# Low weight halves on GpSimd, four past-row pairs a block, rows out earlier and the compressed past kept on chip, in a hybrid conv and sparse-attention decoder step

## The reference, cut to what matters

```python
def even_project(x, w_in):                       # 1024 -> 3352 columns
    h = jnp.einsum('btd,de->bte', x, w_in)
    a_val, a_glu, a_gate, q, kv_c, kv_s, kv_w, g, b_gate = jnp.split(h, offsets, axis=-1)
    u = a_val * jax.nn.sigmoid(a_glu)
    ...
def conv_branch(u_ext, a_gate, conv_w, conv_b, ln_g, ln_b):     # 512 channels, width 31, causal
    y = lax.conv_general_dilated(u_ext, conv_w[:, None, :], (1,), 'VALID', ...) + conv_b
    return jax.nn.silu(layer_norm(y, ln_g, ln_b)) * jax.nn.silu(a_gate)

def compress_kv(kv, w_cmp):                      # 32 rows -> 1, stride 16
    ch = kv[:, :n_ch * CMP_STRIDE].reshape(B, n_ch, CMP_STRIDE, 2, KV_HEADS, HEAD_DIM)
    kc = (jnp.einsum('bnjchd,jchd->bnchd', ch[:, :-1], w_cmp[:CMP_STRIDE])
          + jnp.einsum('bnjchd,jchd->bnchd', ch[:, 1:], w_cmp[CMP_STRIDE:]))
    ...
def nsa_block(q, g, q_pos, kc, vc, kc_end, ks, vs, kw, vw, kw_pos):
    # three branches: compressed blocks, the 16 best blocks of 64 rows, the last 512 rows;
    # o = sigmoid(g)[0] * o_c + sigmoid(g)[1] * o_s + sigmoid(g)[2] * o_w
    ...
def mixer_out(a_out, b_out, b_gate, w_out):
    h = jnp.concatenate([a_out, b_out * jax.nn.silu(b_gate)], axis=-1)
    return jnp.einsum('bte,ed->btd', h, w_out)
```

## Time and profile before

| | us |
|---|---|
| runs | 1334.31, 1334.58, 1342.15; median 1334.58 |
| the profiled execution | 1331.57, span 1329.7 |
| busy: PE | 1182.9 (89%) |
| DVE | 732.0 (55%) |
| POOL | 392.4 (30%) |
| ACT | 376.1 (28%) |

### The profile page before, as it was taken

One profiled execution on the slowest core, in us unless ns is written; L12 is line 12 of the kernel. 1 busy time (PEld: TensorE's weight loads), 2 busy tenths in 40 slices (PEclk: granted clock), 3 DMA queues, 4 the chain that ended last, 5 costly groups with the idle time before them and its releaser, 6 DMA issues.

```text
span 1329.7 us, 17791 instructions
## 1 busy us (share of the span) xinstructions
PE 1182.9 (89%) x7119; PEld 953.6 (72%) x7119; DVE 732.0 (55%) x1394; ACT 376.1 (28%) x791; POOL 392.4 (30%) x352
## 2 busy tenths in 40 slices
PE   5998999979989488899988999799969999978996
PEld 5998999979967244454544545478769999977883
DVE  2566889999934576445454454543435650065332
ACT  2211111111134454544545444511101121143000
POOL 3422200000012653432433323354412222124444
PEclk9998999989989588899999999899979999988998
DMA  7534333112130700040120301432112111041221
GB/s 225 184 108 154 112 96 80 32 32 48 32 157 0 263 11 1 1 159 1 45 114 1 159 1 69 129 106 93 52 52 79 47 47 39 9 145 52 95 95 40
DMA packets 77912, 105.22 MB, mean 79 GB/s; under 512 B 21280, under 2 KB 63912, under 8 KB 76607
## 3 DMA queue, kind: packets, MB, share of 16 engines
q1 hardware_dynamic: 69743, 69.62, 16.8%
q0 software_dynamic: 6016, 33.56, 6.8%
q10 hardware_dynamic: 2080, 1.05, 0.3%
HBM read 91.47 MB, written 17.69 MB: 82 GB/s over the span
## 4 chain that ended last, share of the span: by engine, by line
PE 63%; DVE 23%; ACT 5%; issue 4%; DMA 2%; POOL 1%; SPq 1%; POOLq 0%; ACTq 0%; DVEq 0%
PE PS L1511 15%; PE PS L1648 14%; DVE Y L543 9%; PE PS L648 9%; PE PS L1069 6%; PE PS L950 5%; PE PS L1083 3%; PE PS L640 2%; DVE ACC L495 2%; PE PS L1044 2%; PE PS L1003 2%; DVE WL L272 1%; PE PS L998 1%; ACT PRW L1109 1%; DVE PS L1163 1%
## 5 line engine op out<-in xcount | busy, mean ns | idle before, releaser
L648 PE MATMUL PS<-XH,WH 128*128 128x352 f32 (+1 forms) x648 | 149.2, 335 | 14.4 <-DVE WL L272 10.9
L543 DVE SCALAR_TENSOR_TENSOR Y<-U,SM,Y 128x1024 f32<-128x1024 f32 x120 | 145.9, 1279 | 0.2
L648 PE MATMUL PS<-XL,WH 128*128 128x352 f32 (+1 forms) x648 | 144.2, 327 | 0.0
L648 PE MATMUL PS<-XH,WL 128*128 128x352 f32 (+1 forms) x648 | 144.2, 327 | 0.0
L648 PEld LDWEIGHTS PS<-XH,WH 128*128 128x128 f32 (+1 forms) x648 | 110.0, 190 | 18.1 <-DVE WL L272 12.1
L648 PEld LDWEIGHTS PS<-XL,WH 128*128 128x128 f32 (+1 forms) x648 | 111.3, 189 | 1.4
L648 PEld LDWEIGHTS PS<-XH,WL 128*128 128x128 f32 (+1 forms) x648 | 111.0, 189 | 1.4
L1511 PE MATMUL PS<-WOH,XH 128*128 128x512 f32 (+1 forms) x288 | 94.2, 409 | 13.7 <-POOL WOL L1482 7.3
L495 DVE SCALAR_TENSOR_TENSOR ACC<-PS,SM,ACC 128x508 f32<-128x508 f32 x124 | 84.0, 740 | 40.5 <-PE PS L640 39.1
L950 PE MATMUL PS<-PT,TM 128*64 128x256 f32 x528 | 91.0, 425 | 12.4 <-ACT PT L1100 7.7
L1069 PE MATMUL PS<-KV,Q 64*128 64x512 f32 (+3 forms) x384 | 88.1, 515 | 15.2 <-ACT PRS L1109 12.4
(11 more groups left out here) (289 smaller groups left out, 2122.6 us busy)
## 6 DMA issues: line engine op xcount, KB each, us to landing
WRAW<-in_w_in_even SPq DMA_DIRECT2D x16, 512.0 KB, 4.3
WRAW<-in_w_in_odd SPq DMA_DIRECT2D x16, 512.0 KB, 3.9
XIN<-in_x_prompt SPq DMA_DIRECT2D x8, 512.0 KB, 12.5
WRAW<-in_w_in_even SPq DMA_DIRECT2D x16, 256.0 KB, 3.5
TM<-in_state_win_kv SPq DMA_DIRECT2D x8, 512.0 KB, 7.8
XR<-in_x_prompt SPq DMA_DIRECT2D x8, 512.0 KB, 3.5
layer_out<-R SPq DMA_DIRECT2D x8, 512.0 KB, 2.6
XR<-layer_out SPq DMA_DIRECT2D x8, 512.0 KB, 3.2
```

Source lines behind the costliest of these rows:

```text
L543: ins = v.scalar_tensor_tensor(dst, src, CWT[:, i, t:t + 1], dst, ALU.mult, ALU.add)
L648: ins = pe.matmul(PS[0:mcols, 3 * slot + c, 0:CH], w[:, slot, kk, 0:mcols], x[:, kk, c * CH:(c + 1) * CH], start=(kk == 0 and n == 0), sto ...
```

## The change

- **Low halves.** POOL makes all 27 (before: blocks 0 to 5, 25 and 26; DVE had 19).
- **Pairs.** Four a block, at kk = 0, 2, 4, 6, in blocks 1 to 8. The DVE list has no `low`, and is not cut by blocks any more: behind block 8's pairs come 18 taps, the prompt's compression, 6 taps, the samples' conv, and then all 94 remaining taps.
- **Rows out.** 40 of the transposes stand behind blocks 14 to 18; ACT copies them to new tiles KVROW, KWROW and SROW; SP stores them with the weight loads 21 and 22. Behind the last block 19 transposes are left (the value rows that the attention multiplies by). The DRAM-to-DRAM copies go with load 16, the conv rows with load 25, and DVE's copies of the conv rows, of VC and of the gates go to ACT.
- **Gate block.** It is block 22 (`M_G`), its 9 transposes stand behind block 23, and the masks and GSM are made by POOL ahead of the multiplications of Y.
- **Layer norm.** `mean(0)`, `mean(1)` stand behind block 24 (before: 23), `mean(2)` inside block 25 at kk = 4, `variance(0)` behind block 25, the other two inside block 26, the last, which is now a full one. SQ has five slots for seven, RSTD three for one.
- **Past on chip.** ACT copies KCTS from ACC behind block 19, and 8 transposes (`turn_past`) give VCN; nothing goes to DRAM, and the two steps `vct` go from the attention's order. No engine waits for `s_stored`.
- **Attention's start.** PE waits only for the last block's evacuation. XH and XL of Y (events `H`), the first gather of selected rows and the small tables (`prep`) are woven into `ORDER` from its place 10 on.

```diff
-M_KV, M_Q, M_AG, M_BG = 8, 14, 18, 22
-LOW_DVE = (6, 25)
+M_KV, M_Q, M_AG, M_G, M_BG = 8, 14, 18, 22, 23
+PER_BLOCK = 4
...
@@ SP @@
+                if m == 16:
+                    for dst, src in ((o_win_s[0, :, 0:WIN - DS], state_win_kv[0, :, DS:WIN]), ...):
+                        sp.dma_start(dst, src).then_inc(s_out, 16)
+                if m == 21:
+                    sp.wait_ge(s_rowc, 8)
+                    for dst, c in ((o_kvc_p, 0), (o_kvs_p, 256)):
+                        sp.dma_start(..., KVROW[:, :, c:c + 256]).then_inc(s_rowst, 16)
...
@@ POOL @@
+            for m in range(1, NM + 1):
                 low(po, m)
+                if m < 8:
+                    gather(m)
+            pool_masks(po, link)
             for i in range(4):
                 po.wait_ge(s_ys, i + 1)
                 po.tensor_tensor(Y[:, i, :], Y[:, i, :], AG[i][:, :], ALU.mult).then_inc(s_ya, 1)
...
@@ DVE @@
-            for m in range(LOW_DVE[1]):
-                if m in (2, 4, 6, 8):
-                    glu(m // 2 - 1)
-                mine = range(min(3 * m - 3, NPAIR), min(3 * m, NPAIR)) if m else range(0)
-                ...
-                if m and not mine:
-                    taps(3)
-                    low_next(m + 1)
-                    if m == 14:
-                        compress_prompt()
-                    elif m == 15:
-                        conv_samples()
-                        taps(3)
-                    else:
-                        taps(7)
+            for m in range(1, 9):
+                for n in range(PER_BLOCK):
+                    compress(PER_BLOCK * (m - 1) + n)
+                    if n == 0 and m % 2 == 0:
+                        glu(m // 2 - 1)
+                if m >= 5:
+                    taps(2 if m % 2 else 1)
+            taps(18)
+            compress_prompt()
+            taps(6)
+            conv_samples()
             taps(len(TAPS))
...
@@ PE @@
+            for m in range(14, 19):
+                if m > 14:
+                    one(m)
+                turn_rows(2 * (m - 14))
+                turn_rows(2 * (m - 14) + 1)
+            one(19)
+            turn_past(0)
+            turn_past(1)
...
-            for m in range(21, 24):
-                one(m)
-            pe.wait_ge(s_vc, 1)
-            pe.wait_ge(s_conv, 4)
-            mean(0)
-            mean(1)
-            one(24)
-            mean(2)
-            variance(0)
-            one(25)
-            variance(1)
-            variance(2)
-            one(NM)
+            one(24)
+            pe.wait_ge(s_conv, 4)
+            pe.wait_ge(s_vc, 1)
+            pe.wait_ge(s_gtok, 1)
+            mean(0)
+            mean(1)
+            one(25, ((4, mean, 2),))
+            variance(0)
+            one(NM, ((3, variance, 1), (6, variance, 2)))
...
@@ attention @@
-            pe.wait_ge(s_stdc, 3)
-            pe.wait_ge(s_gtok, 1)
-            for tt in (NTT - 2, NTT - 1):
-                pe.wait_ge(*tm_done(tt))
+            pe.wait_ge(s_ev, 2 + NM + 1)
...
+        for n, x in enumerate([("H", i) for i in range(4)] + [("gather", 0), ("prep",)]):
+            ORDER.insert(FIRST_H + 2 * n, x)
```

More of the change, by code:

```diff
@@ L249, in sp_program @@
+                if m == 25:
+                    sp.wait_ge(s_ue, 2)
+                    sp.dma_start(o_conv_p[0, 0], UROW[0:CW - 1, 0, :]).then_inc(s_urow, 16)
+                    for b in range(DB):
+                        sp.dma_start(o_conv_s[0, b, CW - 1 - DS:CW - 1], UROW[DS * b:DS * b + DS, 1, :]).then_inc(s_urow, 16)
             sp.wait_ge(s_gtok, 1)
@@ L269, in low @@
         def low(eng, m):
-            n = 24 if m == NM else P
+            n = width(m)
             eng.wait_ge(s_wh, m + 1)
@@ L307, in pool_program @@
             gather(0)
[L308 to L313, removed]
-            low(po, 4)
-            gather(4)
-            low(po, 5)
-            for n in range(5, 8):
-                gather(n)
-            for m in range(LOW_DVE[1], NM + 1):
-                po.wait_ge(s_wl, m)
+            for m in range(1, NM + 1):
                 low(po, m)
+                if m < 8:
+                    gather(m)
+            pool_masks(po, link)
             for i in range(4):
@@ L420, in act_program @@
-            for tt in range(0, NTT, 2):
-                act.wait_ge(s_tmt, tt + 1)
-                if tt == NTT - 1:
-                    act.wait_ge(s_urow, 16 * (1 + DB))
-                act.activation(TM[0:ntok(tt), tt, :], turned_kv(tt), ACT.Copy).then_inc(s_tma, 1)
+            for n in (0, 2):
+                act.wait_ge(s_tmt, n + 1)
+                act.activation(*value_rows(n), ACT.Copy).then_inc(s_tma, 1)
+            act.wait_ge(s_tmt, 5)
+            act.activation(TM[0:NSAMP, 8, 384:768], PS[0:NSAMP, 7, 0:384], ACT.Copy).then_inc(s_tma, 1)
@@ L690, in variance, with one @@
                               stop=(i == 3)).then_inc(s_sqr, 1)
-            def one(m):
+            def one(m, between=()):
                 pe.wait_ge(s_wl, m + 1)
@@ L825, in program @@
                    (("gs",), 4000, 600), (("take", ("gs",)), 0, 0), (("pct",), 1500, 300), (("take", ("pct",)), 0, 0)]
-        for a in range(2):
-            SAMPLE += [(("vct", a), 1000, 600), (("take", ("vct", a)), 0, 0)]
         SAMPLE += [(("rank", a, n), 2000, 0) for a in range(2) for n in range(3)]
@@ L1291, in pool_attention, with gather @@
             po.sem_inc(s_masks, 1)
-            po.wait_ge(s_al, 4)
-            for b in range(2):
-                gather(b)
+            po.wait_ge(s_vrow, 48)
+            link(po.memset(GSM[:, :], 0.0))
+            for g in range(GROUP):
+                link(po.affine_select(out=GSM[:, :].rearrange("p (a g t) -> p a g t", g=GROUP, t=DS),
+                                      in_=GSM[:, :].rearrange("p (a g t) -> p a g t", g=GROUP, t=DS),
+                                      compare_op=ALU.not_equal, fill=1.0, base=-DS * g,
+                                      pattern=[[-16, 8], [0, GROUP], [-1, DS]], channel_multiplier=1))
+            po.sem_inc(s_gsm2, 1)
+        def pool_attention(po, link):
+            def gather(b):
+                po.indirect_dma_start(out=RING[:, b % 2, :], out_offset=None, in_=sel_chunks,
+                                      in_offset=bass.IndirectOffsetOnAxis(ap=idx[:, 40 + b:41 + b], axis=0))\
+                    .then_inc(s_ring[b % 2], 16)
             scaled_pairs = 0
```

373 lines of the change are left out of this document (199 added, 174 removed).

## The result

The changed kernel takes **1361.3 us** (median of 4, 1357.5 to 1364.4) against 1334.4 (4 runs): ratio 1.0195, 95% interval 1.0135 to 1.0254. It is **27 us slower**; forecast was 26 us faster. The profiled execution has a span of 1355.7 us.

The account below looks back on a forecast made before the run. DVE's pace in the projection and a gap behind it with PE nearly idle were taken as bounds. Projection -11.3, gap -13.5 and dropped steps -1 gave -26 us: median 1308 us, range 1298 to 1412.

Parts of the forecast that it names:

- What the low halves cost from POOL: Projection: 16 low halves under taps take turns with DVE, each holding it 2.2 us, 35 us; taps end at 371.6.
- Starved: Rival, chance 0.30: under taps no low half gets a turn between two taps; projection ends 83 us later, median 1405.
- partly starved: Rival, chance 0.14: a low half waits several taps, but not all; 1325 to 1380.
- The first stretch: Blocks 1 to 8 with four pairs each: 6 us added for PE's waits, block 8 ends at 173.3.
- The rest of the sum: Projection's end behind the taps, gap and dropped steps: -11.3, -13.5 and -1 us, together -26.
- the forecast's own case: Low halves on POOL take turns with DVE's taps, chance 0.42; last block ends at 411.9, median 1308.
- the case without cost: Rival, chance 0.06: low halves on POOL cost DVE nothing, PE alone sets the pace; projection ends at 403.6, time 1300.
- Gap: Between the projection's end and the attention: shorter chain ahead of exponentials and scores wins 13.5 us (9 to 17).
- DMA: State copies beside weight loads of blocks 17 and 18: a load takes 8 us and fits in 11.5; cost 0 (bound 8).

Follow-up runs that it names:

- e8: Changed kernel plus a tiny one-column memset on VectorE behind every fourth tap from the 44th on, no wait added; 1301.6 us, one run.
- e1: Changed kernel, with VectorE waiting at 13 places in its long stretches of taps until the due low half is done; 1311.2 us, ratio to before 0.984.
- e2: Changed kernel with the low halves of blocks 10 to 25 back on VectorE; 1302.5 us, ratio to before 0.978.
- e6: e2 with the stretch behind the last block reordered: two Y multiplications, XH/XL, first gather and tables come later; 1292.0 us, ratio to before 0.968.
- e11: Changed kernel with the three DRAM-to-DRAM copies issued behind weight load 26 instead of load 16; 1359.5 us, one run.
- e3: Kernel before with all low halves on GpSimd, the three late gathers between them, and nothing else changed; 1336.9 us, ratio 1.003.
- e9: Changed kernel with the tiny VectorE memset only behind taps 48, 64, 80, 96 and 112; 1308.0 us, one run.
- e10: e6's order behind the last block, all low halves on GpSimd, memset behind every fourth tap from the 44th on; 1297.4 us, ratio to before 0.971.
- e4: Changed kernel with 122 taps as a plain addition of two SBUF inputs, without the weight; 1382.4 us, one run.
- e5: Changed kernel with the taps' weight a constant in the instruction instead of read from SBUF; 1381.2 us, one run.

## Why the prediction was wrong

- **The step that failed** is "What the low halves cost from POOL": "They take turns: POOL waits at most one DVE instruction and then holds DVE for 2.1 to 2.2 us. I take this value". For those that got a turn the price was right (a tap of 3.42 us instead of 1.27). But not all get one: two waited over 14 and 48 boundaries between taps, and PE waited 59.3 us for them. I laid, the one meeting with taps, aside for seven meetings with short runs of VectorE, in which at most two of its large instructions had finished since it last stood idle. The row told it: 4.87 us, asked for in the 16th of 16 instructions back to back since a copy from PSUM.
- **"Starved" at 0.30 was closer in mechanism**, too pessimistic in extent: it starved every low half, put the two waits of 25 and 65 where 9.8 and 49.5 were measured, and one of 14 that did not come. The time lay between both cases, in "partly starved", 0.14.
- **The first stretch** held: block 8 forecast to end at 173.3, and it ends at 171.9, where VectorE's last additions are done too. Pairs cost PE 3.7 us of waiting, against 6 assumed.
- **The rest of the sum** held once the turns were there. e8 is the forecast's own case, GpSimd with its turns: taps end at 365.8 (forecast 371.6), the last block at 405.2 (411.9), and the time is 1301.6 (1308). With VectorE's waits (e1) the last block ends at 416.5. For the case without cost 403.6 was forecast; e2 has 399.9, and e6, with the same projection, 404.4.
- **Gap**: exponential at +8.5 (forecast 10.1), first turning of probabilities at +19.3 (16), samples' scores at +33.6 (28). From the last block's end to the output projection it was 442.1 us before (865.3 - 423.2) and is 426.1 (891.4 - 465.3): 16 us less, where 14.5 was forecast. What I missed is the slow scaling beside XL's subtractions and the 6.8 us for the tables. Why the layer still won more than forecast, though the turning and the samples' scores came later, these runs don't explain.
- **DMA**: the copies do delay load 17, by more than "8 and fits": 21.6 us to landing, which made a rounding copy 1.5 us late (4.4 in e2). It cost PE nothing by itself, as e2's 190.50 of 190.50 shows, and e11 shows that it did not set off the starvation.
- **The skill's rule.** The Trainium skill, "SBUF — State Buffer", section "SBUF: two separate sides", has the shared pair of ports held for one instruction by whoever starts first. The turns up to 243 us agree with it (2.6 us at 185.73, and a tap of 3.42). The 60.6 us over 48 boundaries do not: here the measurement decides.

Sum: the last block ends 42.1 us later than before (465.3 - 423.2). Of this 59.3 are the two waits and 5.0 the slow blocks behind them (14.54 + 13.52 - 2 x 11.54), so that the rest of the projection is 22.2 shorter, near e2's 23.3 (423.2 - 399.9). Less 16 in the gap this is +26, as measured between the profiled executions.

## What to carry to other kernels

Before work moves to GpSimd beside a long run of VectorE instructions, count how many follow one another without a break where the request falls, not how the two shared elsewhere in the kernel. If it must stay there, give VectorE a break every few instructions, even a memset of one column, from the first long run on (low half 11 starved ahead of the first memset), or a wait at the right place. One row of the very pair of instructions outweighs many of similar ones.

## What the runs showed of the hardware

The counts are for weighted taps (1.20 us apart, both inputs in SBUF) and a subtraction of 128x1024 on GpSimd, over before, after, e1, e3, e8, e9, e10 and e11. They go by the taps that VectorE had finished since its last break or GpSimd's last turn:

| taps finished at the request | low halves that got their turn at the next boundary |
|---|---|
| 0 to 4 | all |
| 5 to 7 | 15 of 20 |
| 8 to 15 | none of 10; they waited for the next break, however far |

Left out are requests ahead of the small multiplications of the samples' conv (most waited 3.3 us, over 8 of them) and those of e1 that met one of VectorE's 13 waits or the boundary of the 62nd tap. The five that starved at 5 to 7 are low half 11 in e9 and e10, one more in e9 (the row at 290.17), one in e3 (26.7 us) and the last one of e1.

A turn resets the count, and blocks 11.5 us apart make it 7; the transposes behind blocks 14 and 15 stretch the distance past 12 us, and the count to 8 or 9. That fits where starvation began in the changed kernel. It is an edge, not a rule: low half 11, asked for with seven taps finished and 0.95 us into the eighth, got through in after, e8 and e11 and starved in e9 and e10. What in the chip counts to seven or so, the runs don't show, and with the faster taps of e4 and e5 one starved after two. Nor was it tried how short an idle gap may be (at the boundary of the 62nd tap it is 0.15 us), or another instruction than a subtraction on GpSimd.
